# Late modulation chunks taken out of the output projection and put beside the differential-attention heads

## The reference, cut to what matters

```
mod = silu(c) @ w_mod + b_mod          # c: one vector for the prompt, one for the sample; w_mod 2048 x 12288
sh_a, sc_a, gt_a, sh_f, sc_f, gt_f = split(mod, 6)
h = rmsnorm(x, g_attn) * (1 + sc_a) + sh_a
z = h @ w_in                            # q, k, v of 8 A heads and of the B heads
oa = differential attention of the 8 A heads (two softmax maps each), then a per-head RMSNorm
ob = sliding-window attention of 16 B heads, 4 kv heads, with a sink
x = x + gt_a * (concat(oa, ob) @ w_out)
h2 = rmsnorm(x, g_ffn) * (1 + sc_f) + sh_f
u = causal conv(h2 @ w_up); x = x + gt_f * ((silu(u_gate) * u_val) @ w_down)
y = rmsnorm(x, g_final)
```

## Time and profile before

| | |
|---|---|
| Time, median of 3 runs | 2734.76 us (2732.97 to 2735.49) |
| The profiled execution | 2732.63 us, of which its span is 2730.9 us |
| PE busy | 2620.5 us (96%) |
| DVE busy | 1558.8 us (57%) |
| ACT busy | 957.5 us (35%) |
| POOL busy | 544.7 us (20%) |
| Mean granted PE clock | 0.985 |

### The profile page before, as it was taken

One profiled execution on the slowest core, in us unless ns is written; L12 is line 12 of the kernel. 1 busy time (PEld: TensorE's weight loads), 2 busy tenths in 40 slices (PEclk: granted clock), 3 DMA queues, 4 the chain that ended last, 5 costly groups with the idle time before them and its releaser, 6 DMA issues.

```text
span 2730.9 us, 50066 instructions
## 1 busy us (share of the span) xinstructions
PE 2620.5 (96%) x19783; PEld 2445.0 (90%) x19783; DVE 1558.8 (57%) x2873; ACT 957.5 (35%) x1974; POOL 544.7 (20%) x477
## 2 busy tenths in 40 slices
PE   7999999999999996999999999999999999999997
PEld 2268889898988995999999999999999999999997
DVE  1369889864457887854443544444444444345454
ACT  2236666654344336422222222222222222222224
POOL 1057777751003543310000000000000000000003
PEclk9999999999999998999999999999999999999998
DMA  8866556551216652533323232332332233232321
GB/s 291 294 202 184 184 174 183 182 145 51 66 40 188 169 165 70 155 108 93 93 79 93 81 90 82 90 88 83 93 92 72 87 93 91 81 93 79 93 93 69
DMA packets 416205, 324.91 MB, mean 119 GB/s; under 512 B 44410, under 2 KB 360218, under 8 KB 414880
## 3 DMA queue, kind: packets, MB, share of 16 engines
q1 hardware_dynamic: 410032, 302.55, 37.3%
q0 software_dynamic: 5248, 14.56, 1.7%
q10 hardware_dynamic: 688, 4.47, 0.4%
HBM read 307.67 MB, written 14.07 MB: 118 GB/s over the span
## 4 chain that ended last, share of the span: by engine, by line
PE 81%; DVE 8%; DMA 3%; issue 3%; POOL 2%; ACT 2%; SPq 1%; ACTq 0%; DVEq 0%; POOLq 0%
PE ps L1565 24%; PE ps L1567 23%; PE ps L1566 23%; DVE late_f L1261 3%; PE ps L1539 3%; PE ps L1654 2%; PE ps L1620 2%; DMA w_raw<-in_w_mod 2%; DMA w_raw<-in_w_out 2%; POOL oT L696 1%; PE ps L1638 1%; SPq L536 1%; DVE oT L1261 1%; ACT w_hi L798 1%; PE ps L1576 1%
## 5 line engine op out<-in xcount | busy, mean ns | idle before, releaser
L1565 PE MATMUL ps<-x_hi,w_hi 128*128 128x272 f32 x4480 | 1319.0, 294 | 53.7 <-DVE w_lo L1155 24.7
L1567 PE MATMUL ps<-x_hi,w_lo 128*128 128x272 f32 x4480 | 1302.9, 291 | 0.0
L1566 PE MATMUL ps<-x_lo,w_hi 128*128 128x272 f32 x4480 | 1293.5, 289 | 0.0
L1565 PEld LDWEIGHTS ps<-x_hi,w_hi 128*128 128x128 f32 x4480 | 850.3, 190 | 72.5 <-issue 32.2
L1566 PEld LDWEIGHTS ps<-x_lo,w_hi 128*128 128x128 f32 x4480 | 851.7, 190 | 0.0
L1567 PEld LDWEIGHTS ps<-x_hi,w_lo 128*128 128x128 f32 x4480 | 849.0, 190 | 0.0
L1155 DVE TENSOR_TENSOR w_lo<-w_raw,w_hi 128x1024 fp32r<-128x1024 f32 x368 | 459.0, 1276 | 341.0 <-ACT w_hi L798 340.6
L798 ACT ACTIVATE w_hi<-w_raw 128x1024 fp32r<-128x1024 f32 x368 | 375.6, 1056 | 715.3 <-PE ps L1567 574.1
L1566 PE MATMUL ps<-y_lo,w_hi 128*128 128x272 f32 x1408 | 407.2, 289 | 0.0
L1565 PE MATMUL ps<-y_hi,w_hi 128*128 128x272 f32 x1408 | 405.8, 288 | 0.0
L1567 PE MATMUL ps<-y_hi,w_lo 128*128 128x272 f32 x1408 | 405.0, 288 | 0.0
(11 more groups left out here) (194 smaller groups left out, 2081.6 us busy)
## 6 DMA issues: line engine op xcount, KB each, us to landing
w_raw<-in_w_mod SPq DMA_DIRECT2D x192, 512.0 KB, 4.6
w_raw<-in_w_up SPq DMA_DIRECT2D x176, 512.0 KB, 4.4
w_raw<-in_w_down SPq DMA_DIRECT2D x88, 512.0 KB, 4.7
w_raw<-in_w_in SPq DMA_DIRECT2D x56, 512.0 KB, 3.9
w_raw<-in_w_in SPq DMA_DIRECT2D x32, 256.0 KB, 3.7
w_raw<-in_w_out SPq DMA_DIRECT2D x16, 512.0 KB, 5.5
w_raw<-in_w_out SPq DMA_DIRECT2D x64, 128.0 KB, 3.9
x_transposed<-xT SPq DMA_DIRECT2D x4, 1088.0 KB, 8.1
```

What stands on the lines that cost most here:

```text
L1565: pe.matmul(out[:, 0:n], hi_w, hi_x, start=first, stop=False)
L1566: pe.matmul(out[:, 0:n], hi_w, lo_x, start=False, stop=False)
L1567: return pe.matmul(out[:, 0:n], lo_w, hi_x, start=False, stop=last)
```

## The change

Two constants. Twelve groups instead of ten are placed by the first half of the table, two instead of four by the second. The work of a chunk stays as it is.

```diff
-LATE1 = 10 * LPG
-LATE2 = 4 * LPG
+LATE1 = 12 * LPG
+LATE2 = 2 * LPG
 LATE3 = 2 * LPG
 LSUM = 2
 LATE_AT = [2 + n * 48 // LATE1 for n in range(LATE1)] + [ZH + 1 + n * 28 // LATE2 for n in range(LATE2)]
```

## The result

| | Before | After |
|---|---|---|
| Median | 2735.12 us (2732.97 to 2737.93, 4 runs) | 2768.25 us (2761.46 to 2774.39, 4 runs) |
| Ratio, 95% interval | | 1.012 (1.0108 to 1.0132) |
| The profiled execution, its span | 2732.63, 2730.9 us | 2764.47, 2762.7 us |

The changed kernel is 33 us slower. I had forecast 2742 and a range that ended at 2755. The sign was right, the size was not.

What follows compares the result with a forecast made beforehand. PE's own work was taken to bound both stages, with DVE able to make it wait. +14 us beside the A heads and -6.5 in the output projection gave +7.5 on 2732.6, plus 2.1 for the median: 2742, range 2730 to 2755.

Steps and rivals of the forecast that it cites:

- the output projection: Stage that 16 chunks leave: PE's waits for w_lo nearly all go, -6.5 us; stage shorter by 10 with columns.
- the forecast of 17: Beside the A heads: PE waiting of 9.0, 2.7 and 5.5 us, before the adjustments that lead to +14 us.
- The price: DVE's cost of one added chunk beside the A heads: 3.15 us, lower end 1.5, upper end 3.9.
- The hiding: Beside the A heads, ten chunks cost 31.5 us against 32.2 idle on DVE, four fifths usable; 5.5 us left.
- The slack of 1.35 us: Beside the A heads, half 8: from ACT's copy ending to PE coming, about what DVE may fall back before PE waits.
- The small scaling: DVE's L1296 beside the A heads: goes from 0.17 to 0.75 us beside POOL's adds; 30 x 0.60 = 18 us waiting.
- Columns: Column sums in four halves, 0.95 us of PE each, move from output projection to A heads; nothing in sum.
- `o_norm`: PE's 4.5 us of waits beside the A heads: half goes; POOL's later roots add 2 us for eight heads.
- (a): Rival: DVE and POOL take turns throughout, a chunk costs 3.9 us, stage grows 24 to 30; about 2755, chance 0.14.
- (b): Rival: lag swallowed beside the A heads, a chunk costs 2.4 us, 38 against 41 idle; 2733, chance 0.24.
- (c): Rival: faster, multiply-adds fall where DVE waits, 1.5 us each, output projection gives 6.5 or more; 2728, chance 0.12.
- (d): Rival: output projection gives back little, -2 instead of -6.5 us, its odd halves' weight loads late; 2747, chance 0.08.

Runs made afterwards that it cites:

- add_memset: Changed kernel with each of POOL's late adds replaced by two memsets of the same 128x512 that read nothing; 2699.9 us.
- The two reorderings: Each on the changed kernel: ACT's eviction ahead of the w_hi copy, 2762.2 us; DVE's next maximum ahead of the half's second late chunk, 2757.5 us.
- after_max_first: Changed kernel with DVE taking the next turn's maximum before the half's second late chunk; 2757.5 us.
- load_narrow: Changed kernel with each late chunk's load cut from 512 to 64 columns, same number of loads; 2772.3 us.

## Why the prediction was wrong

The kind was right: PE's work does not change, DVE is the engine without room, each engine lengthens the other's instructions, the new waits of PE stand beside the A heads, the output projection gives back about what was said. What was to be seen in the profile was partly met: L1261's mean above 1.25 (1.32) yes, L696's above 1.5 no (1.49), new waits of PE yes, for `w_lo` at most 1 us no (3.2), DVE busy 45 to 55 us more no (59). The waits were to be some 9 us for `probsT` in halves 7 to 13. There PE is idle 2.1 us against 1.9 before; the first twelve halves have 7.0 us more of idle time, but mostly in half 6 and in halves 14 and 15, and what PE waits for most is L901.

**The sum of the stage, term by term.** The 16 chunks were to cost DVE 50 us, 17 of them visible, 33 in its idle time. DVE's time (stage less its idle) went from 372.9 to 432.1: 59 us, or 3.7 a chunk. Its idle time went from 46.5 to 29.0: only 17.5 us were hidden. 59.2 - 17.5 = 41.7, the measured growth. Against the forecast of 17 the price accounts for 9 us, the hiding for 16.

**The price** was 3.15 us, with 3.9 as upper end; 3.7 was measured. The wait of all rose by a factor of 1.39 (92 to 128 us), where I had the product of both loads, 1.29. For each of the 146 and 176 adds inside the stage that is 0.63 and 0.73 us. And 3.7 is a mean of 3.1 for the first of the two groups and 4.3 for the second: what I called the upper end, 3.9, is none. That fits a new add lengthening the multiply-adds that were there too: the median of all of them went from 0.756 to 1.490 us. Of the two prices the one with the full alternation was the nearer, and I had chosen the one by the means of rows 4.

**The hiding is the step that failed most:** "the other ten cost 31.5 against 32.2 idle ... I count four fifths of it as usable: 5.5 us". DVE's idle time is the waiting for PE and ACT inside a turn; it is still there, 29 us of it, when DVE is the bound. With DVE's 432 us of need against PE's own 414 (the stage with no waits, `add_memset`) there was nothing left to hide in. The halves from 16 to 52, where those ten chunks are and the two from 427 to 479, grew by 26 us, where the sum had 5.5 + 2.7. With eleven groups DVE's need is 397 us, and with the 15 to 34 us that stay idle in the kernels with eleven or twelve groups over 48 halves and whole adds it is 412 to 431: at PE's floor or a little over. The twelfth group adds 35 us to the need and the idle time falls by 2.7 only, so nearly all of it comes on top. That is the cliff.

**The slack of 1.35 us** was read at the wrong place. In the earlier trace rows I took ACT's copy (L888) as the releaser of PE's values and counted from its end. PE also needs the bank that L901 empties, and on ACT the copy of `w_hi` and L901 itself stand between. In the kernel before, in half 8:

```profile
219.11 1.05 ACT L798 ACTIVATE w_hi<-w_raw 128x1024 fp32r<-128x1024 f32 x1
220.06 0.35 ACT L901 ACTIVATE oT<-ps,gsub 128x128 f32<-128x128 f32 x1
```

The eviction ended at 220.41 and PE began its values at 220.55: the true slack was 0.14 us and not 1.35. The two reorderings of this chain gave 6 and 11 us, so it was a smaller error than the hiding.

**The clock was not a term at all.** I priced waits at their length. Here 21.6 us of new waits brought 30.7 us at 1.2 GHz and so 15 more. How much follows varies: with 23.5 us of new waits `after_max_first` had 10.2 us of it, and it was still at 454 us. How long the stage would be without the dips isn't shown: they lengthen PE's part of a half, and that gives DVE time too. Counted on PE's side, the forecast's 14 us of stalls were 21.6, 7.6 more, and the clock, at nothing in the sum, was 15.3. This and the count by price and hiding are two counts of the same 42 us; no run takes the dips away alone and so says which is to be blamed for how much.

**The small scaling** L1296 was priced at 0.60 us of waiting for each, 18 us in all, all of it put down to the adds. In `add_memset` its mean in the stage is still 0.34 us and not the 0.17 that I took for it alone, against 0.73 in the kernel before. So a good part of it, but not all, is the adds'.

**What was right or harmless.** Columns +3.8 us, as forecast. `o_norm`: 4.5 before, 5.5 now; neither the gain of 2 nor the loss of 2 is seen. The loads cost nothing (`load_narrow`), and ACT's added products alone cost nothing (`add_memset` has them, and PE is idle for 0.0 us). The output projection from half 72 to 103 is 8.6 us shorter, where 10 were forecast. PE's idle time there went from 9.5 to 4.5, and the columns are 3.8; this kernel has 8.2 us at 1.2 GHz there against 1.3, which should cost 3.5, so that some 3 us of gain are not accounted for by these rows.

**The rivals.** (a), the full lock, had the nearest price and kept 2755, because it too hid a good part: 33 of 62 us. With 3.7 us a chunk, 17.5 hidden and the forecast's own 6.5 for the output projection the sum is 2732.6 + 41.7 - 6.5 + 2.1 = 2770; this only puts the measured terms in, it is no forecast. (b) and (c) needed a price below 2.5 us, and a chunk cost DVE 3.1 and 4.3. (d) is out: the output projection gave back 8.6 us and more, not 2.

## What to carry to other kernels

When an engine that is 90% busy beside a full PE gets more work, don't count all of its idle time as room: 15 to 34 us of 427 to 466 stayed idle here in every kernel with eleven or twelve groups over 48 halves and whole adds. What is over the rest was paid nearly in full, and PE's stalls brought half-clock time on top. Where a multiply-add on DVE and an add on POOL both read SBUF, look at the median against the minimum of the DVE line. Here it stood near the minimum with ten groups (0.756 against 0.729 us) and far from it with twelve (1.490 against 0.736); that it can serve as a warning elsewhere is not shown. For the slack of a step of PE take every instruction that the releasing engine has queued up to the last one that PE needs, not the first.

## What the runs showed of the hardware

- DVE's two-input instructions wait for POOL's reading adds for some 92 us (146 adds) and 128 us (176 adds) in this stage, by the estimate of the table; beside POOL's memsets of the same tiles the multiply-adds take 0.752 us at the median against 1.490. With memsets or narrow adds everywhere the changed kernel takes 2700 us.
- The small scaling of the maximum, 128x2 with one tensor input, takes longer beside reading adds as well: its mean in the stage is 0.73 us in the kernel before and 0.34 in `add_memset`, its shortest 0.17 in both.
- Cutting an add of 128x512 in two and in four pieces costs POOL 1.96 and 2.43 us instead of 1.49, each measured beside DVE's work.
- After PE had been idle 2.6 of 13 us, 2.25 of them in one stall, the granted clock fell to 1.2 GHz for most of the following 4 us, with PE busy throughout. All eight dips of the stage began 1 to 2 us after the end of a stall of 1.5 to 2.3 us. Waits of 1.5 and 1.9 us in the kernel before brought no dip in this stage.
